# Sparse attention: a head's bias row, in two pieces, behind the values of its first and second step

## The reference, cut to what matters

```
logits = (einsum('bqhr,bqkr->bqhk', qa, c_sel) + einsum('bqhe,bqke->bqhk', qr, kr_sel)) * scale
p = masked_softmax(logits, valid[:, :, None, :]).astype(c_sel.dtype)
return jnp.einsum('bqhk,bqkr->bqhr', p, c_sel)
...
bias = rel_bias[rel_bucket(pos_k[None, :] - pos_q[:, None])]
```

## Time and profile before

| | us |
|---|---|
| time, median of 3 runs (2311.2 to 2312.06) | 2311.52 |
| time of the profiled execution | 2311.79 |
| its span | 2310.5 |
| PE busy in the span | 2238.2 |
| DVE busy | 1378.6 |
| ACT busy | 562.1 |
| the row matmuls (16 records), between 276.4 and 337.5 us | 8.2 |

### The profile page before, as it was taken

How to read it: one execution, slowest core, us unless ns; L and a number is a source line. 1 busy time by engine, 2 the same in 40 slices (tenths; PEclk the granted TensorE clock), 3 DMA queues, 4 the chain that set the end, 5 groups by cost and what they waited for, 6 DMA issues and landing times.

```text
span 2310.5 us, 29663 instructions
## 1 busy us (share of the span) xinstructions
PE 2238.2 (97%) x11026; PEld 1620.2 (70%) x11026; DVE 1378.6 (60%) x3539; ACT 562.1 (24%) x1421; POOL 64.2 (3%) x79
## 2 busy tenths in 40 slices
PE   7999999999999999999999999999999999999997
PEld 6776678888888886557888888888767643333333
DVE  6777637665665658997765656767776422222224
ACT  2223332100010113774210100233463111111110
POOL 0000000000000000000000000000010011111010
PEclk9999969999999999999999999999999999999999
DMA  5211013222222321001322222222104899999997
GB/s 208 74 56 46 7 54 110 91 90 82 84 91 91 122 77 43 1 1 37 91 91 81 85 91 91 85 98 74 55 19 175 325 421 422 425 422 423 425 423 309
DMA packets 60207, 346.54 MB, mean 150 GB/s; under 512 B 9248, under 2 KB 10144, under 8 KB 42208
## 3 DMA queue, kind: packets, MB, share of 16 engines
q1 hardware_dynamic: 55360, 335.03, 38.8%
q0 software_dynamic: 3840, 6.46, 0.7%
q10 hardware_dynamic: 864, 3.15, 0.3%
HBM read 337.59 MB, written 17.30 MB: 154 GB/s over the span
## 4 chain that ended last, share of the span: by engine, by line
PE 74%; DMA 7%; DVE 4%; issue 1%; ACT 1%; SPq 0%; DVEq 0%; POOLq 0%; ACTq 0%
PE bank L622 26%; PE bank L628 7%; PE bank L643 7%; PE bank L635 7%; DMA places<-in_experts 7%; PE bank L3004 6%; PE bank L3012 3%; PE bank L611 2%; PE bank L2964 1%; PE bank L1090 1%; PE bank L1075 1%; PE bank L1102 1%; DVE exps L2240 1%; PE bank L2977 1%; PE bank L1297 1%
## 5 line engine op out<-in xcount | busy, mean ns | idle before, releaser
L3004 PE MATMUL bank<-places,xT 128*64 128x512 f32 x824 | 183.8, 594 | 13.5 <-DMA places<-in_experts 13.5
L3211 DVE TENSOR_SCALAR square<-bank,mt 128x256 f32<-128x256 f32 x32 | 15.5, 484 | 286.2 <-ACT rope L3116 286.2
L3004 PEld LDWEIGHTS bank<-places,xT 128*64 128x64 f32 x824 | 59.4, 137 | 132.3 <-issue 118.4
L1932 DVE TENSOR_TENSOR third<-first,bank 128x256 f32<-128x256 f32 x106 | 44.7, 421 | 151.0 <-PE bank L622 150.3
L622 PE MATMUL bank<-u,ring 128*128 128x256 f32 x540 | 130.1, 381 | 1.1 <-DVE y_ab L1966 1.1
L622 PE MATMUL bank<-h,ring 128*128 128x256 f32 x512 | 121.0, 379 | 0.0
L622 PE MATMUL bank<-h_sums,w_sum 128*128 128x256 f32 x512 | 121.0, 379 | 0.0
L622 PEld LDWEIGHTS bank<-u,ring 128*128 128x128 f32 x540 | 101.3, 190 | 17.3 <-issue 2.8
L622 PE MATMUL bank<-u_mlp_sums,w_sum 128*128 128x256 f32 x480 | 113.4, 379 | 0.0
L622 PE MATMUL bank<-u_mlp,ring 128*128 128x256 f32 x480 | 113.4, 379 | 0.0
L1481 ACT ACTIVATE h<-relu 128x512 f32<-128x512 f32 x64 | 40.3, 630 | 273.7 <-DVE relu L2114 249.2
(11 more groups left out here) (545 smaller groups left out, 4361.9 us busy)
## 6 DMA issues: line engine op xcount, KB each, us to landing
places<-in_experts SPq DMA_DIRECT2D x56, 2048.0 KB, 35.1
ring<-in_dense SPq DMA_DIRECT2D x216, 512.0 KB, 4.2
places<-in_experts SPq DMA_DIRECT2D x40, 1024.0 KB, 24.4
x<-in_experts SPq DMA_DIRECT2D x12, 1024.0 KB, 36.8
w<-in_experts SPq DMA_DIRECT2D x10, 1024.0 KB, 30.5
consts<-in_experts SPq DMA_DIRECT2D x10, 1024.0 KB, 31.2
x<-in_experts SPq DMA_DIRECT2D x4, 2048.0 KB, 31.7
consts<-in_consts SPq DMA_DIRECT2D x1, 2310.5 KB, 16.6
```

The lines of the kernel that those rows point to most:

```text
L1932: dve.tensor_tensor(u3, u2, part[7], ALU.add).then_inc(s["shared"], 1)
L3004: ins = k.pe.matmul(bank[a * CAP:(a + 1) * CAP, :], xT[:, kk % 4, kk // 4, :], w[:, (2 * (kk % 2) + a) * EH:(2 * (kk % 2) + a + 1) * EH], ...
```

## The change

Both engines that touch the row pieces issue them at other places of the same loop; nothing else changes. Piece (h,0) now stands at the end of step h.0 and piece (h,1) at the end of step h.1, behind the values. ACT takes piece (h,0) at the start of its step h.1 and piece (h,1) at the start of its step h.2, ahead of the exponentials.

```
-        if 1 <= m <= 4 and at == 0:
-            pe_row(k, m - 1, 1)
         if len(FOX) <= step - 2 < len(SOFT):
             pe_soft_turn(k, step - 2)
         if len(FOX) <= step - 3 < len(SOFT):
             pe_soft_values(k, step - 3, k.ch6)
-        if m < 4 and at == 3:
-            pe_row(k, m, 0)
+        if m < 4 and at < 2:
+            pe_row(k, m, at)
...
-        if 1 <= m <= 4 and at == 0:
-            act_take(k, k.ch7, ("row", m - 1, 1), k.row[m - 1][:, T:LV], k.ch7.bank[:, 0:LV - T])
+        if m < 4 and at == 1:
+            if m >= 2:
+                act.wait_ge(s["row_out"], 16 * (m - 1))
+            act_take(k, k.ch7, ("row", m, 0), k.row[m][:, 0:T], k.ch7.bank)
+        if m < 4 and at == 2:
+            act_take(k, k.ch7, ("row", m, 1), k.row[m][:, T:LV], k.ch7.bank[:, 0:LV - T])
...
-        if m < 4 and at == 3:
-            if m >= 2:
-                act.wait_ge(s["row_out"], 16 * (m - 1))
-            act_take(k, k.ch7, ("row", m, 0), k.row[m][:, 0:T], k.ch7.bank)
```

## The result

| | before | changed |
|---|---|---|
| median, 7 runs of each on the first chips | 2307.32 (2299.58 to 2312.06) | 2294.59 (2290.37 to 2301.49) |
| profiled execution | 2311.79, span 2310.5 | 2292.23, span 2290.9 |

The ratio of the runs is 0.995 with an interval of 0.9927 to 0.9972: faster, by 0.3 to 0.7%, a small gain but clear of the noise. The difference of the medians is 12.7 us, that of the two profiled executions 19.6, against 18.9 forecast. Both kernels differ from execution to execution by more than 10 us, which the first three runs of before, all within 0.9 us, had not shown.

The account below looks back on a forecast made before the run. PE was taken as the bound, with short in-order waits at head boundaries and a clock falling behind them. Gains 17.60 and 1.96 less loss 0.66 made 18.90 us; 2311.52 - 18.90 = 2292.6 us, range 2289 to 2305.

Parts of the forecast that it names:

- The mechanism: Sparse-attention head boundaries: PE idles for ACT's in-order copies and the clock falls behind; 2.57 us are waits, some 16 clock.
- 1.25 us: Boundary of heads 1 and 2, step 2.0: new PE wait for ACT to free bank 4, left standing by the change.
- Head period: One head of the passage at full clock, both row pieces in it: 12.82 us.
- New waits: Middle stretch, replacing removed waits: 1.25 us at heads 1 and 2, 0.15 at 2 and 3, 0.3, 0.08; together 1.78.
- The middle stretch: Step 1.0 to step 4.0: from 57.84 us to 40.24 if the clock stays full, a gain of 17.60.
- Start: Steps 0.0 to 0.3: piece (0,0) waits 0.28 us and a 128-wide piece of 0.38 moves in; loss 0.66 us.
- Tail: Step 4.0 to step 4.1: from 4.54 us, mostly at half clock, to 2.58; gain 1.96 us.
- A: The forecast itself: clock stays full through the passage; 2292.6 us, own range 2290 to 2295; chance 0.62.
- rival B: Clock falls once all the same, behind the 1.25 us wait: 2297.1 or 2301.7 us, up to 2305; chance 0.20.
- C: No change to speak of: fall lasting to the tail, 2313 us, or clock follows something else, 2309; chance 0.13.
- the sum by the waits alone: Whole passage, if the clock does not follow such short gaps: a gain of 2.57 us only.
- D: Slower: clock falls in head 0 or early in head 1 and stays down to the tail; 2325.5 us, chance 0.05.

Follow-up runs that it names:

- Experiment 2: Kernel before with fill matmuls between piece (h,0) and the store's wait, eight in step 1.3, five in 2.3 and 3.3; 2296.18 us, ratio 0.9951.
- experiments 4 and 5: Changed kernel with seven instead of two fill matmuls ahead of the first store, 2295.09 us; changed kernel with VectorE's sums moved to the tail, 2294.29, or early, 2291.11.
- spread: Changed kernel with sums in the tail, rows 0 and 1 pieces in head 0, the others in steps 3.0, 3.1, 4.0, 4.1, less fill; 2290.83 us.
- spread with the sums early: The kernel spread with VectorE's three blocks of sums in steps 1.0, 2.0 and 3.0 instead; 2291.23 us, ratio 0.9916.

## Why the prediction was right

**The mechanism.** It held in each part: a gap of PE at the head boundaries, made by ACT's order; the clock that falls behind it; the change takes the gap away. Experiment 2 shows that the falls follow the gaps and not the place of the pieces: with the gaps filled the clock is full for the whole passage. What it does not show is that every gap brings a fall. Over the passages of all 13 traces 12 gaps of 1.15 to 2.18 us begin at full clock, and the clock falls behind nine of them; behind a gap of 0.78 us or less it never does, unless one of 1.15 has gone just before. Whether one comes behind 1.25 us was therefore a matter of chances, as the prediction has it. Nor does the fall stand right behind the wait, as the prediction read it: in the first trace of before the clock falls at 290.9, 1.4 us into the first gap, and at 311.4, 1.3 us behind the end of the second; in the changed kernel's two it falls some 2 us behind the end.

**The sum, step by step,** for an execution without a fall, which the first trace of after is:
- Head period: forecast 12.82, measured (317.93 - 278.46 - 2.10 of waits) / 3 = 12.46. Most of the difference lies in the last turns and values of a head: step 1.2's took 286.40 - 284.07 = 2.33 us in the kernel before and 287.99 - 285.89 = 2.10 here, the last values 0.49 and 0.40. Why they are shorter is not shown.
- New waits: 1.78 forecast; 0.04 + 1.39 + 0.36 + 0.31 = 2.10. The middle stretch thus takes 39.47 us, and the gain is 57.84 - 39.47 = 18.37 where 17.60 was forecast.
- Start: loss 0.66 forecast. Steps 0.0 to 0.3 take 278.46 - 266.90 = 11.56 instead of 10.56, so 1.00: the wait is 0.35 and not 0.28, and the 128-wide piece takes 0.41. The rest is a term that the forecast lacked: the logits of 0.0 and 0.1, 0.86 us in one group before, take 0.49 + 0.64 = 1.13 with the piece between them.
- Tail: 320.32 - 317.93 = 2.39, forecast 2.58, so the gain is 2.15 instead of 1.96.
- Together 347.90 - 328.44 = 19.46 us earlier at the projection, and the end follows (1962.6 and 1962.5 us behind it).

**What was mis-sized** is the term on which most of the sum rests, and the step is the base of it: "the profiled execution took 2311.79 us, 0.27 above the median of the runs". I took its 37.6 us of half clock as every execution's of before, and A as every execution's of the changed kernel. Both vary. Before has 37.6 and 17.1 us of half clock in its passage in two traces; changed has 0 in one and 17.1 in two. Medians of one chip are 13.2 us apart (2310.75 of 35 runs and 2297.52), those of the first runs 12.7, not 18.9. That the time forecast, 2292.6, came within 2 us of the measured 2294.59 is in part luck: the base was 4.2 us too high against the median of all seven runs (2307.32) and the gain 6.2 too large, and the two errors go against each other. That the first profiled execution was one without a fall, 19.6 us below that of before, is luck too. The measured median lies in A's own range; single executions need the wider one, with rival B at 2297.1 and 2301.7: the other two that were profiled took 2303.47 and 2300.83. B's chance of 0.20 was too small as a share of executions (two of three traces; by the times some 11 of 26 runs). Its cause, the 1.25 us wait left standing, is supported by experiments 4 and 5: without that wait no fall stands there in any of three traces.

**The rivals.** C's first half, a fall that lasts to the tail, was not seen in the changed kernel, though the kernel before with its sums moved comes near (34.1 us). C's second half (the clock follows something else) falls with experiment 2, and with it the sum by the waits alone, to which the rule on long idle gaps in the Trainium skill (TensorE: Matmul & The Clock Gate, "Why this matters for your kernels") would have led. Falls stand here behind gaps of 2.18, 1.96, 1.38, 1.17, 1.15 and, in three traces of 13, 1.03 us; the measurement decides against the rule. The other passage of that page of the Trainium skill, "A second HAM failure mode: psum-queue depth-cycling", on short idles between groups of matmuls that make the clock swing, is nearer to these traces, though here single gaps do it. D did not occur: the clock was full in head 0 in all 13 traces, in spread too, with less fill.

## What to carry to other kernels

Where PE has a short in-order wait, read the granted clock behind it: the wait may cost ten times its own length. Behind the 1.15 us gap of the first trace half clock lasted 27.3 us, at 0.44 us for each of them an estimated 12 us. Either take away what makes the wait (the order on the releasing engine), or put fill matmuls into it, or do both; shortening it may bring nothing. Look at what follows the gap too. A gap of 1.66 us at 217 us is in all 13 traces; the clock fell behind it in nine, but each time for 3.4 us only, with 512-wide matmuls behind the gap. In the passage, with narrower ones, the falls lasted 3.4 to 34.1 us. That the width makes this difference is not shown; no run changed it alone. And ask for several executions before a sum is made against one trace, since the same instructions at the same times ran with and without the fall.

## What the runs showed of the hardware that I had not expected

- The same program, with PE's starts in the passage equal to within 0.1 us up to 292.8, kept 1.00 behind a wait of 1.39 us in one execution and fell to 0.50 behind one of 1.38 in another.
- Once down in the passage, the clock stayed down for 3.4 to 34.1 us, behind the same 1.15 us gap of the kernel before 27.3 us in one execution and 6.8 in another, although PE was busy nearly all the time (17.00 of 17.00 us in one stretch, 33.00 of 33.80 in another) with logits of 64 rows, transposes, and 64-column values matmuls. Why these don't bring it back sooner was not tested.
- Gaps of 0.36 us at the same places were followed by no fall in any trace, nor were two of 0.78 in spread with the sums early.
- A gap's length alone does not decide. Behind the 1.66 us gap that stands at 1749.96 us in the first trace of before the clock stayed full in all 13 traces; behind that of 1.66 at 217 it fell in nine. Behind the eight gaps of 0.91 to 1.04 us that each trace has between 879 and 1042 us, ahead of turns, it never fell. What sets them apart was not tested.
